# Four slots for split weights and three for raw ones, in a four-layer hybrid model kernel

## What is computed

```python
# first kind, twice
h = rms_norm(x, norm_w[l]);  p = h @ w_in[l]                 # 2048 x 6668
y = concat(window_attention(...), conformer_conv(...), gated_deltanet(...))
x = x + y @ w_out[l]                                         # 2048 x 2048
# second kind, twice
h = rmsnorm(x, ln1_g[l]);    p = h @ w_in_2[l]               # 2048 x 6176
y = concat(diff_attention(...), gated_linear_attention(...), retention(...))
x = x + y @ w_o_2[l]                                         # 2048 x 2048
h = rmsnorm(x, ln2_g[l])
u = conv3(h @ w_up_2[l]) + conv_b                            # 2048 x 11264
x = x + (a * silu(g)) @ w_down_2[l]                          # 5632 x 2048
return rmsnorm(x, final_g)
```

## Time and profile before

| what | before |
|---|---|
| median of the runs | 3772.99 us |
| time of the profiled execution | 3774.01 us |
| its span, first to last instruction | 3772.2 us |
| PE busy | 3541.7 us (94%) |
| DVE busy | 2320.3 us (62%) |
| ACT busy | 1863.3 us (49%) |
| mean granted TensorE clock | 0.981 |
| DMA, mean over the span | 153 GB/s |

### The profile page before, as it was taken

One profiled execution on the slowest core, in us unless ns is written; L12 is line 12 of the kernel. 1 busy time (PEld: TensorE's weight loads), 2 busy tenths in 40 slices (PEclk: granted clock), 3 DMA queues, 4 the chain that ended last, 5 costly groups with the idle time before them and its releaser, 6 DMA issues.

```text
span 3772.2 us, 42968 instructions
## 1 busy us (share of the span) xinstructions
PE 3541.7 (94%) x16794; PEld 2862.4 (76%) x16794; DVE 2320.3 (62%) x3204; ACT 1863.3 (49%) x2544; POOL 54.5 (1%) x101
## 2 busy tenths in 40 slices
PE   7899889899889998899999999999888999999998
PEld 5688668788668776678778788787666888878876
DVE  5487566577565655556666656656555565665665
ACT  4634545643545345455444445453555554544444
POOL 3000000000000000000000000000000000000000
PEclk9999999999999999999999999999999999999999
DMA  7433436433436334455565565563344666555554
GB/s 210 117 110 103 128 103 198 128 107 104 131 95 200 118 116 129 117 167 183 180 188 180 179 190 181 181 181 98 122 131 120 190 190 188 180 183 185 179 184 151
DMA packets 398523, 577.70 MB, mean 153 GB/s; under 512 B 25185, under 2 KB 222297, under 8 KB 397680
## 3 DMA queue, kind: packets, MB, share of 16 engines
q1 hardware_dynamic: 392544, 557.93, 48.4%
q0 software_dynamic: 5328, 15.83, 1.4%
q10 hardware_dynamic: 448, 1.18, 0.1%
HBM read 570.65 MB, written 4.19 MB: 152 GB/s over the span
## 4 chain that ended last, share of the span: by engine, by line
PE 76%; DVE 14%; ACT 7%; issue 3%; DMA 0%; DVEq 0%; ACTq 0%; SPq 0%
PE PS L695 73%; DVE WL L1779 4%; PE PS L692 3%; ACT WH L1269 2%; DVE AR L1919 1%; DVE AR L2417 1%; DVE AR L2422 1%; DVE X L1789 1%; DVE SM L2319 1%; DVE AR L2317 1%; DVE AR L2331 0%; ACT L1530 0%; DVE AR L2429 0%; DVE AR L2245 0%; DVE AR L2427 0%
## 5 line engine op out<-in xcount | busy, mean ns | idle before, releaser
L1779 DVE TENSOR_TENSOR WL<-RAW,WH 128x1024 fp32r<-128x1024 f32 x1056 | 1285.9, 1223 | 1015.9 <-ACT WH L1269 1015.3
L1269 ACT ACTIVATE WH<-RAW 128x1024 fp32r<-128x1024 f32 x1056 | 1103.7, 1055 | 957.3 <-PE PS L695 951.2
L695 PE MATMUL PS<-WH,Ah 128*128 128x512 f32 x3520 | 1431.8, 407 | 63.9 <-DVE WL L1779 36.7
L695 PE MATMUL PS<-WH,Al 128*128 128x512 f32 x3520 | 1386.3, 394 | 0.0
L695 PE MATMUL PS<-WL,Ah 128*128 128x512 f32 x3520 | 1386.0, 394 | 0.0
L695 PEld LDWEIGHTS PS<-WH,Ah 128*128 128x128 f32 x3520 | 670.8, 191 | 238.9 <-issue 47.5
L695 PEld LDWEIGHTS PS<-WL,Ah 128*128 128x128 f32 x3520 | 669.1, 190 | 144.6
L695 PEld LDWEIGHTS PS<-WH,Al 128*128 128x128 f32 x3520 | 670.8, 191 | 136.1 <-issue 5.8
L695 PE MATMUL PS<-AR 128*128 128x128 f32 (+5 forms) x2208 | 312.5, 294 | 19.3 <-DVE GT L2202 7.0
L695 PEld LDWEIGHTS PS<-AR 128*128 128x128 f32 (+3 forms) x2208 | 266.0, 192 | 71.8 <-PE PS L695 25.8
L695 PE MATMUL PS<-WH,Zh 128*128 128x512 f32 x704 | 280.6, 399 | 27.2 <-DVE WL L1779 27.2
(11 more groups left out here) (312 smaller groups left out, 2090.2 us busy)
## 6 DMA issues: line engine op xcount, KB each, us to landing
RAW<-in_w_in SPq DMA_DIRECT2D x368, 512.0 KB, 3.7
RAW<-in_w_up SPq DMA_DIRECT2D x704, 256.0 KB, 3.1
RAW<-in_w_down SPq DMA_DIRECT2D x176, 512.0 KB, 4.5
RAW<-in_w_out SPq DMA_DIRECT2D x64, 512.0 KB, 3.6
RAW<-in_w_o SPq DMA_DIRECT2D x64, 512.0 KB, 3.9
RAW<-in_w_in SPq DMA_DIRECT2D x64, 256.0 KB, 3.0
AR<-in_c POOLq DMA_DIRECT2D x2, 1600.0 KB, 8.9
AR<-bias_scratch POOLq DMA_DIRECT2D x16, 192.0 KB, 4.6
```

The source lines that it names most:

```text
L695: return T.matmul(o, lhs, rhs, start=start, stop=stop, skip_group_check=True)
L1269: act(WH[:, j % NW, 0:n], raw_view(j), ACT.Copy).then_inc(*w_hi())
L1779: tt(WL[:, j % NW, 0:w], raw_view(j), WH[:, j % NW, 0:w].bitcast(F32), SUB).then_inc(*w_lo())
```

## The change

The number of raw slots goes from four to three, and that of split slots from three to four. A split slot costs twice the room of a raw one (WH and WL), so 4 KB per partition have to be found: the arena AR, the tables C1, PRM and PB are cut to what they hold. The scratch row JUNK (squares in `prepare`) moves into AR 12288, where other stages have their buffers; the narrow evacuation gets a place of its own (NARROW); the k copies and rotary scratch (KS, RT) move to ZA; RSQ and EPS move too. The masks c2 are loaded over the new place of JUNK, so GpSimd now waits for the squares of that round first.

```diff
-NRAW, NW = 4, 3
+NRAW, NW = 3, 4
...
-        AR = sb("AR", [128, 17408])
+        AR = sb("AR", [128, 16896])
...
-        C1 = sb("C1", [128, 1552])
-        PRM = sb("PRM", [128, 1264])
-        PB = sb("PB", [128, 1024])
+        C1 = sb("C1", [128, 1544])
+        PRM = sb("PRM", [128, 1258])
+        PB = sb("PB", [128, 864])
...
-        EPS = C1[:, 1544:1545]
+        EPS = SM[:, 766:767]
...
-        ROPE = PB[:, 860:892]
+        ROPE = PB[:, 832:864]
...
-        JUNK = ar(16896, 512)
+        JUNK, NARROW = ar(12288, 512), ar(10240, 256)
...
-        KS, PW = ar(16896, 2, 256), ar(14336, 4, 512)
-        RT = [ar(16896 + 128 * i, 128).rearrange("p (h d) -> p h d", d=8) for i in R4]
+        KS, PW = za(1024, 2, 256), ar(14336, 4, 512)
+        RT = [za(1024 + 128 * i, 128).rearrange("p (h d) -> p h d", d=8) for i in R4]
...
-        CT, TP, RO_, RSQ = ar(15360, 2, 512), ar(15360, 2, 512), ar(16384, 512), ar(16896, 512)
+        CT, TP, RO_, RSQ = ar(15360, 2, 512), ar(15360, 2, 512), ar(16384, 512), ar(12800, 512)
...
-                    ins = tr(PS[:, 2 * s + k, 256:256 + n], JUNK[0:n, 128 * k:128 * k + 128], n)
+                    ins = tr(PS[:, 2 * s + k, 256:256 + n], NARROW[0:n, 128 * k:128 * k + 128], n)
...
-                act(JUNK[0:n, 0:256], PS[0:n, 2 * s, 0:256], ACT.Copy).then_inc(*n_act(key + ".copy"))
+                act(NARROW[0:n, 0:256], PS[0:n, 2 * s, 0:256], ACT.Copy).then_inc(*n_act(key + ".copy"))
...
                 narrow("2", l, "ga")
+                G.wait_ge(*p_sum.at(2 + 2 * l))
                 G.dma_start(AR[:, 11264:14464], a["c2"]).then_inc(c2_in, 16)
```

## The result

| | before | after |
|---|---|---|
| median of the runs, us | 3772.7 (3770.4 to 3774.8, 4 runs) | 3728.9 (3728.2 to 3732.3, 4 runs) |
| profiled execution, us (its span) | 3774.0 (3772.2) | 3729.5 (3727.7) |
| mean granted clock of TensorE | 0.981 | 0.979 |

The ratio is 0.9889, 95% interval 0.9876 to 0.9902: 43.8 us less, where 50.4 were forecast. Beside other runs of the kernel before, the same kernel later gave 0.9900 (0.9885 to 0.9915). The forecast of 3723 us is 5.9 us too low, and the time lies inside the range of 3706 to 3748. The sum did not come out because all of its terms were right.

A forecast was written before the change was run, and what follows sets the result against it. PE was taken as the bound, busy 3541.7 of 3772.2 us, so gains come from its gaps: 35.2 + 5.1 + 5.4 + 6.8 - 2.1 = 50.4 us, giving 3723 us. The 8-in-10 range was 3706 to 3748.

The forecast's parts named there:

- The FFN: Groups with up and down chunks: late subtractions no longer stall PE, 1.76 us a group, 20 groups, 35.2 us gained.
- Two signs: Right if PE's list shows 0.1 to 0.2 us waits for L1789; wrong if ACT's RAW waits exceed 2 us in the FFN.
- The moves: Scratch at other addresses changes no size and no engine: zero cost.
- qkv chunks: DVE's convolution holds up ACT's tanh and the next split; three waits vanish, 3 x 1.7 = 5.1 us gained.
- `mixer_a`: At its start three waits add up to one lateness; a slot takes off 2.7 us in each of two layers, 5.4 us.
- `gla`: At its start PE gets one tile ahead, then still waits for L2260; 3.4 us gained in each layer, 6.8 us.
- Where nothing was counted: Head norms of `mixer_c`, the short WL wait ahead of `diff` and the very first wait: no gain.
- The start: Raw loads are released a tile later at kernel start, so the sixth tile loses 2.1 us (bounds 0 and 4).
- That the FFN's wait turns into another: Rival: PE stops a tile further on in the FFN, only the mixers' 15 us left: 3759 us, chance 0.12.
- The raw ring as a bound: Rival: the raw ring becomes the bound of the FFN, from a landing of 5.9 us: 3836 us, chance 0.04.
- The clock: Rival: more tiles in the starts of `gla` and `mixer_a` run at the low level, 13.6 us: 3737 us, chance 0.08.
- That the slot does nothing: Rival: what was late is late by order and not by slots: 3773 us, chance 0.05.

The follow-up runs named there:

- the kernel with Zh in place: The changed kernel with the storage of Zh, Zl and ZA allocated ahead of C1, so Zh and Zl begin at a multiple of 64 bytes: 3725.4 us, ratio 0.9881.

## Why the prediction was right, and the step that failed

**The FFN** was right in every piece of its mechanism: both stalls vanish, and the add to x of the second down chunk is what comes next. Its 1.76 us a group is what the kernel with Zh in place gives (1.75). In the change itself it is 1.42, because of the step that comes next. Two signs of it were badly chosen: waits for L1789 are in no list of waits, since a delay of 0.19 us shows only in the starts; and waits of ACT for raw loads over 2 us do stand in the FFN (up to 4.8), with no harm to PE.

**The moves: the step that failed.** "Scratch at other addresses changes no size and no engine: zero." The scratch did cost nothing. But the room came from narrower tensors too, and the step never asked what else is allocated behind them. The whole miss is 6.6 us; the other terms, which were off by up to 3 us in both directions, nearly cancel. Nothing in the trace of before could have priced this step, but the diff named all the sizes. The Trainium skill, "TensorE: Matmul & The Clock Gate", section "Back-to-back issue gap", gives the spacing of matmuls by columns and clock, with no term for where an operand lies, and by it the moves would have changed nothing; the runs show 0.234 us instead of 0.227 at the same clock of 1.00, so here the measurement decides. The Trainium skill, "SBUF — State Buffer", section "Operand start alignment", only demands a multiple of the element size, and says itself that it is about what is allowed and not about speed.

**qkv chunks, `mixer_a`, `gla`** came out at 5.7, 5.4 and 6.4 us against 5.1, 5.4 and 6.8. In `gla` PE stops for L2260 as foreseen: that result ends at 1274.07 and its matmuls start at 1274.22. That is 11.1 us earlier than before, 7.7 of it from the tiles ahead, so 3.4 us are of this place. The granted clock in the stretch behind the first stall is 0.66, the same as in the earlier trace rows:

```profile
1262.50:1267.50 5.00, 5.00 (x16) 3.79 (x16) 4.90 (x4) 0.92 (x1) 0.00 (x0) 0.66 0.37 108
```

**Where nothing was counted.** In the head norms the tiles come 1.5 us earlier, PE then stands longer, and the next tile gives back 3.0 or 3.1, of which 1.6 returns: zero, as said. The same holds ahead of `diff`.

**The start** cost 2.5 us at the sixth tile (2.1 forecast). At the fourteenth it was 5.3, and 1.9 with the same slots in the kernel with Zh in place. The difference is one tile at the low clock behind a wait for L1881:

```profile
71.50:78.50 7.00, 7.00 (x15) 4.02 (x14) 4.23 (x5) 0.65 (x2) 1.56 (x3) 0.51 0.82 256
```

```profile
71.19 1.76 PE L695 MATMUL PS<-AR 32*128 32x512 f32 x2 [2.35 <-DVE AR L1881]
```

A granted clock of 0.51 is the level of 1.2 GHz, and the engine had stood 2.35 us just before. In the kernel with Zh in place the same tile took 4.0 us and not 6.5, and the clock stayed at 1.00, although PE had stood 2.46 us for the same line. In the second profiled execution of the change the loss at the fourteenth tile was 3.6 us. So this part of the price is the clock's, and it differs from one execution to the next; what decides it is not shown.

**The rivals.** That the FFN's wait turns into another has fallen: the one that comes next is 0.19 us. The raw ring as a bound is real, but lies a slot further down (4112 us with two slots). The clock moved by 0.002 of its mean; single places lost or won up to 3 us by it, as above, but not where the rival put it. That the slot does nothing has fallen with the terms above. **GpSimd** stood 32.6 us in all, 17.7 at most, and the masks of layer 0 are issued at 1186.22, 88 us ahead of their use at 1274.22; only "a few us" was too short: for the masks of layer 0 GpSimd stood 17.7 us.

## What to carry to other kernels

A further slot for a prepared operand removed lateness up to one tile's time here, place by place; read the starts, and ask at each place what is late next. Price a slot that is given up at the places where its ring starts and restarts, not only in steady work, and remember that a ring above the consumer's pace can cost far more than its excess, as with two raw slots here.
